# Block sums of the down-projection weights made on the chip by GpSimd instead of in DRAM, in a one-core RetNet/GLA/ConvFFN decoder step

## What is computed

```python
n2 = rmsnorm(h, ln2)
up = n2 @ w_up
u, vv = up[..., :D_FF], up[..., D_FF:]
uc, conv_tail = causal_dwconv(u, conv_prev, conv_w, conv_b)
h = h + (jax.nn.gelu(uc, approximate=False) * vv) @ w_down     # D_FF = 2816, D_MODEL = 1024
```

## Time and profile before

| | us |
|---|---|
| runs of the kernel | 831.44, 833.9, 834.17 (median 833.9) |
| the profiled execution | 830.95 |
| its span | 829.0 |
| PE busy | 816.9 (99%) |
| DVE busy | 590.1 (71%) |
| ACT busy | 375.0 (45%) |
| POOL busy | 219.4 (26%) |
| HBM read, written | 145.31 MB, 58.40 MB |

### The profile page before, as it was taken

How to read it: one execution, slowest core, us unless ns; L and a number is a source line. 1 busy time by engine, 2 the same in 40 slices (tenths; PEclk the granted TensorE clock), 3 DMA queues, 4 the chain that set the end, 5 groups by cost and what they waited for, 6 DMA issues and landing times.

```text
span 829.0 us, 15746 instructions
## 1 busy us (share of the span) xinstructions
PE 816.9 (99%) x6544; PEld 806.2 (97%) x6544; DVE 590.1 (71%) x765; ACT 375.0 (45%) x524; POOL 219.4 (26%) x258
## 2 busy tenths in 40 slices
PE   8999999999999999999999999999999999999996
PEld 8999999999999999999999999999999999999996
DVE  5464678477898886766558877777777756878973
ACT  5553234232354554534343544444434424544574
POOL 4017236444325500000430433333233322000020
PEclk9999999999999999999999999999999999999998
DMA  9769968983325974528899598589699873555522
GB/s 271 215 204 176 277 200 174 189 238 124 110 96 105 202 256 140 173 96 265 149 250 273 91 259 217 155 194 192 247 205 210 223 173 120 181 175 175 175 64 108
DMA packets 167889, 152.27 MB, mean 184 GB/s; under 512 B 6677, under 2 KB 155881, under 8 KB 167804
## 3 DMA queue, kind: packets, MB, share of 16 engines
q1 hardware_dynamic: 121612, 109.73, 42.4%
q0 software_dynamic: 46048, 41.04, 28.9%
q10 hardware_dynamic: 160, 0.53, 0.2%
HBM read 145.31 MB, written 58.40 MB: 246 GB/s over the span
## 4 chain that ended last, share of the span: by engine, by line
PE 93%; DVE 4%; issue 1%; DMA 1%; ACT 0%; SPq 0%; DVEq 0%; ACTq 0%
PE mm L2024 51%; PE ax L2317 14%; PE mm L2431 8%; PE ax L2431 6%; PE ax L2043 6%; PE mm L2317 4%; PE ax L2048 2%; PE mm L2104 1%; DVE grs L1443 1%; DMA x_nat<-in_x_prompt 1%; DVE wlo L1433 1%; PE mm L2036 0%; DVE s0g L1613 0%; DVE ylo L1691 0%; DVE wlo L1703 0%
## 5 line engine op out<-in xcount | busy, mean ns | idle before, releaser
L2024 PE MATMUL mm<-nhi,whi 128*128 128x272 f32 x928 | 196.4, 293 | 0.6 <-ACT gqk L1009 0.6
L2024 PE MATMUL mm<-nhi,wlo 128*128 128x272 f32 x928 | 192.5, 289 | 0.0
L2024 PE MATMUL mm<-nlo,whi 128*128 128x272 f32 x928 | 192.1, 288 | 0.0
L1009 ACT ACTIVATE whi<-raw 128x1024 fp32r<-128x1024 f32 (+3 forms) x112 | 128.5, 1182 | 70.1 <-PE mm L2024 38.5
L2024 PEld LDWEIGHTS mm<-nhi,whi 128*128 128x128 f32 x928 | 146.9, 189 | 2.8 <-issue 1.2
L2024 PEld LDWEIGHTS mm<-nlo,whi 128*128 128x128 f32 x928 | 146.5, 189 | 0.0
L2024 PEld LDWEIGHTS mm<-nhi,wlo 128*128 128x128 f32 x928 | 145.6, 190 | 0.0
L1703 DVE TENSOR_TENSOR wlo<-raw,whi 128x1024 fp32r<-128x1024 f32 (+1 forms) x78 | 84.4, 1123 | 5.9 <-ACT whi L1009 3.4
L1433 DVE TENSOR_TENSOR wlo<-raw,whi 128x2048 fp32r<-128x2048 f32 x27 | 64.7, 2398 | 16.1 <-ACT whi L1009 16.1
L940 POOL DMA_DIRECT2D v_sums<-in_w_up x24 | 30.8, 4229 | 117.4 <-DVE mlo L1774 116.9
L1009 ACT ACTIVATE whi<-ring 128x1408 fp32r<-128x1408 f32 x25 | 34.6, 1382 | 44.1 <-PE ax L2431 24.0
(11 more groups left out here) (390 smaller groups left out, 1989.3 us busy)
## 6 DMA issues: line engine op xcount, KB each, us to landing
raw<-in_w_in SPq DMA_DIRECT2D x36, 512.0 KB, 4.9
raw<-in_w_up SPq DMA_DIRECT2D x36, 512.0 KB, 7.9
ring<-w_sums SPq DMA_DIRECT2D x16, 704.0 KB, 4.2
w_sums<-in_w_down SPq DMA_DIRECT2D x12, 704.0 KB, 10.9
w_sums<-in_w_down POOLq DMA_DIRECT2D x12, 704.0 KB, 10.8
ring<-in_w_down SPq DMA_DIRECT2D x9, 704.0 KB, 4.5
v_sums<-in_w_up SPq DMA_DIRECT2D x24, 256.0 KB, 7.0
v_sums<-in_w_up POOLq DMA_DIRECT2D x24, 256.0 KB, 14.0
```

The source lines that it names most:

```text
L1009: return act.activation(out, in_, func, **kw).then_inc(done, 1)
L2024: ins = pe.matmul(mm[:, 2 * j + a, 0:HALF], w, x[:, kx, HALF * a:HALF * (a + 1)], start=first and n == 0 and m == 0, stop=last and n == le ...
```

## The change

S_1 alone is still built in DRAM (four copies by SP at the first two up-projection units, four accumulating DMAs by POOL). The other three sums are made in SBUF. The blocks (0,0) stay where product 0 read them (`kept[0..3]`: the two `raw` slots and two slots of the region of the ring), and POOL adds a streamed block to each with one `tensor_tensor` of 128x1408: first (0,1), which makes S_3 (product 2), then (1,1), which makes S_2 (product 3), then (1,0), which makes S_4 (product 5). Each add waits until the previous content of `kept[m]` has been split (`lo_ready`) and until the streamed block has landed. The blocks come through a ring of four slots (`ring`, the fourth in the region of the convolution's tiles), in the order of `STREAM`; products 1, 4 and 6 are split straight from that ring, and (1,1) is loaded twice. `kept[3]` takes the last block of product 6. The other edits of the same diff move `osq[0]` and make ACT's first two `fin` rows wait for the last sum, because of the fourth ring slot.

```diff
-RING = 5
+RING = 4
-    ring = [at(f"ring{i}", [P, KH, P], a0 + i * AB) for i in range(RING)]
+    ring = [at(f"ring{i}", [P, KH, P], a0 + i * AB) for i in range(RING - 1)]
+    kept = first[:] + [at(f"kept{i}", [P, KH, P], a0 + (RING - 3 + i) * AB) for i in (2, 3)]
...
-    w_sums = nc.dram_tensor("w_sums", [4, P, MD, KH, P], F32).ap()
+    w_sums = nc.dram_tensor("w_sums", [P, MD, KH, P], F32).ap()
...
+    ring.append(at("ring3", [P, KH, P], f + T))
...
+    STREAM = [("s1", 0), ("s1", 1), ("01", 0), ("s1", 2), ("01", 1), ("s1", 3), ("01", 2), ("01", 3)]
+    STREAM += [(b, m) for b in ("11", "10", "11 last") for m in range(MD)]
...
     def source(u):
-        if u < 3:
-            return first[u], (first2_in, 16)
-        i = (u - 3) % RING
-        return ring[i], (ring_in[i], 16 * ((u - 3) // RING + 1))
+        p, m = divmod(u, MD)
+        if p == 0:
+            return (first[2], (first2_in, 16)) if m == 2 else (kept[3], (kept_in[3], 16))
+        if p in (1, 4, 6):
+            return streamed({1: "s1", 4: "10", 6: "11 last"}[p], m)
+        return kept[m], (sum_made, {2: 0, 3: MD, 5: 2 * MD}[p] + m + 1)
...
+        def stream_load(n):
+            name, m = STREAM[n]
+            if RING <= n < 8 or n == 9:
+                old = STREAM[n - RING]
+                if old[0] == "s1":
+                    sp.wait_ge(lo_ready, U_DOWN + MD + old[1] + 1)
+                else:
+                    sp.wait_ge(sum_made, old[1] + 1)
+            elif n in (8, 10, 11):
+                sp.wait_ge(sum_made, STREAM[n - RING][1] + 1)
+            elif 12 <= n < 16:
+                sp.wait_ge(sum_made, MD + m + 1)
+            elif 16 <= n < 19:
+                sp.wait_ge(lo_ready, U_DOWN + 4 * MD + m + 1)
+                sp.wait_ge(sum_made, 2 * MD + m + 1)
+            elif n == 19:
+                sp.wait_ge(lo_ready, U_DOWN + 5 * MD + m + 1)
...
+        sp.dma_start(kept[3][:, :, :], w_block(0, 0, 3)).then_inc(kept_in[3], 16)
+        for n in range(3):
+            stream_load(n)
+        for j in range(2):
+            sp.wait_ge(drained[j], FD[j])
+        sp.wait_ge(ext_saved, KF)
+        stream_load(3)
+        sp.dma_start(kept[2][:, :, :], w_block(0, 0, 2)).then_inc(kept_in[2], 16)
...
+        for n in range(4, len(STREAM)):
+            stream_load(n)
...
         for i in range(KF // 2):
             up_pair(i)
-            if i < 3:
-                weight_sum(S_3, ((0, 1), (2,), (3,))[i], (0, 1))
...
+            if i == 3:
+                pool.wait_ge(sum_begun, 16 * MD)
+            if i in (3, 4):
+                for m in (2 * (i - 3), 2 * (i - 3) + 1):
+                    pool.dma_start(w_sums[:, m], w_block(1, 1, m), accum_op=ALU.add).then_inc(sum_done, 16)
+
+        def sum_block(m, split_before, block):
+            b, (arrived, count) = streamed(block, m)
+            pool.wait_ge(lo_ready, U_DOWN + split_before + m + 1)
+            pool.wait_ge(arrived, count)
+            pool.tensor_tensor(kept[m][:, :, :], kept[m][:, :, :], b[:, :, :], ALU.add).then_inc(sum_made, 1)
+
+        for m in range(MD):
+            if m == 2:
+                pool.wait_ge(kept_in[2], 16)
+            sum_block(m, 0, "01")
+        for m in range(MD):
+            sum_block(m, 2 * MD, "11")
+        for m in range(MD):
+            sum_block(m, 3 * MD, "10")
...
                 if f >= 2:
                     aux_wait_filled(act, ("y", f - 2))
+                else:
+                    act.wait_ge(sum_made, 3 * MD)
```

More of the change, by code:

```diff
@@ L371, in build @@
     facc = at("facc", [P, NT], f)
-    osq = [at("osq0", [P, NT], f + 3 * T), at("osq1", [P, NT], a0 + 5 * AB + D_MODEL * 4)]
+    ring.append(at("ring3", [P, KH, P], f + T))
+    assert T + AB <= 4544 + 2 * T
+    osq = [at("osq0", [P, NT], 3 * UB + AB), at("osq1", [P, NT], a0 + 5 * AB + D_MODEL * 4)]
+    assert AB + T <= UB
     fin = [at(f"fin{i}", [P, NT], f + (1 + i) * T) for i in range(2)]
@@ L417, in build @@
     part_done, part_added = sem("part_done"), sem("part_added")
-    sum_begun = [sem(f"sum_begun{i}") for i in range(4)]
-    sum_done = [sem(f"sum_done{i}") for i in range(4)]
+    sum_begun, sum_done = sem("sum_begun"), sem("sum_done")
     ring_in = [sem(f"ring_in{i}") for i in range(RING)]
+    kept_in = [None, None, sem("kept_in2"), sem("kept_in3")]
+    sum_made = sem("sum_made")
     first2_in = sem("first2_in")
@@ L490, in piece_at @@
         return (n // MD + 1, n % MD)
-    S_1, S_3, S_2, S_4 = range(4)
-    A_OF = ((0, 0), S_1, S_3, S_2, (1, 0), S_4, (1, 1))
     W_DOWN = A["w_down"][0].rearrange("(k p) n -> p k n", p=P)
@@ L498, in w_block, with streamed @@
         return W_DOWN[:, KH * kh:KH * (kh + 1), P * (MD * mh + m):P * (MD * mh + m + 1)]
-    def source(u):
-        if u < 3:
-            return first[u], (first2_in, 16)
-        i = (u - 3) % RING
-        return ring[i], (ring_in[i], 16 * ((u - 3) // RING + 1))
+    STREAM = [("s1", 0), ("s1", 1), ("01", 0), ("s1", 2), ("01", 1), ("s1", 3), ("01", 2), ("01", 3)]
+    STREAM += [(b, m) for b in ("11", "10", "11 last") for m in range(MD)]
+    def streamed(name, m):
+        n = STREAM.index((name, m))
+        if (name, m) == ("11 last", MD - 1):
+            return kept[3], (kept_in[3], 32)
+        return ring[n % RING], (ring_in[n % RING], 16 * (n // RING + 1))
+    def source(u):
+        p, m = divmod(u, MD)
[4 more added lines that the diff above has]
+        return kept[m], (sum_made, {2: 0, 3: MD, 5: 2 * MD}[p] + m + 1)
     def added(f, h):
@@ L677, in cols @@
             return w[:, 0:4, bass.ds(c, UC)], w[:, 4:8, bass.ds(c, UC)]
-        begun = [(i, m) for i in (S_3, S_1, S_4) for m in range(MD)]
         def begin_sums(n):
-            for i, m in begun[2 * n:2 * n + 2]:
-                sp.dma_start(w_sums[i, :, m], w_block(*{S_1: (0, 1), S_3: (0, 0), S_4: (1, 0)}[i], m)).then_inc(sum_begun[i], 16)
+            for m in (2 * n, 2 * n + 1):
+                sp.dma_start(w_sums[:, m], w_block(0, 1, m)).then_inc(sum_begun, 16)
         gs_copies = [(G_3, (0, 0)), (G_1, (0, 1)), (G_4, (1, 0))]
@@ L732, in _ @@
             load((U_WO + n) % 2, U_WO + n - 1, *cols(w_o, UC * n))
-            if n % 2 == 1:
-                begin_sums(n // 2)
         for n, (kind, i) in enumerate(UPS):
@@ L743, in _ @@
                 block_load(u, kind, w_up, D_FF + UC * i, v_sums[:, i - 1])
-            if kind == "u" and i < 4:
-                begin_sums(2 + i)
+            if kind == "u" and i < 2:
+                begin_sums(i)
         for m in range(2):
@@ L751, in _ @@
         sp.dma_start(first[2][:, :, :], w_block(0, 0, 2)).then_inc(first2_in, 16)
[L753 to L761, removed]
-            else:
-                w = w_block(*A_OF[p], m)
-            sp.dma_start(ring[i][:, :, :], w).then_inc(ring_in[i], 16)
+        def stream_load(n):
[15 more added lines that the diff above has]
+                sp.wait_ge(lo_ready, U_DOWN + 5 * MD + m + 1)
+            if name == "s1":
+                if m == 0:
+                    sp.wait_ge(sum_done, 16 * MD)
+                w = w_sums[:, m]
+            else:
+                w = w_block(int(name[0]), int(name[1]), m)
+            to, (arrived, _) = streamed(name, m)
+            sp.dma_start(to[:, :, :], w).then_inc(arrived, 16)
         for j in range(2):
             sp.wait_ge(filled[j], FD[j])
-        for u in range(3, 3 + RING):
-            ring_load(u)
+        sp.dma_start(kept[3][:, :, :], w_block(0, 0, 3)).then_inc(kept_in[3], 16)
[6 more added lines that the diff above has]
+        sp.dma_start(kept[2][:, :, :], w_block(0, 0, 2)).then_inc(kept_in[2], 16)
         for i in range(3):
@@ L775, in _ @@
             sp.dma_start(O[7][0].rearrange("b r d -> (b r) d")[:, c], tail_nat[r + 2:r + 18, 0:n]).then_inc(conv_out, 16)
-        for u in range(3 + RING, PARTS):
-            ring_load(u)
+        for n in range(4, len(STREAM)):
+            stream_load(n)
         yp = O[0][0].rearrange("(j p) d -> p j d", p=P)
@@ L951, in _ @@
         v_weight_sum(G_4, all_sums, lambda i: v_sum(G_2, i))
[L953 to L958, removed]
         def up_pair(i):
```

## The result

The changed kernel takes 852.7 us (median; 851.6 to 853.1) against 833.9 of the kernel before: a ratio of 1.0234, 95% interval 1.0218 to 1.0250, slower. 851.0 was forecast, with 836 to 861 as the range. The profiled execution took 853.1 us, its span is 850.6 us against 829.0. A fourth run of the kernel before, at 1337.7 us, is left out of its median.

The account below looks back on a forecast made before the run. TensorE alone was taken to bound the kernel from 383 us. 830.95+9.7+8.8 gave 849.5 us on the profiled execution, 852.4 on the median of the runs; the forecast was put between, at 851.0, range 836 to 861.

Parts of the forecast that it names:

- step 1: Up projection: removing 8 of SP's copies and 16 of POOL's DMAs gains 0 us, since TensorE doesn't wait there.
- step 5: Down projection, other edits: loads, the S_1 block and the `fin` rows stay hidden, 0 us; slowest landing would cost 3.2 us.
- What the engines do to each other: DVE's and POOL's two-input SBUF instructions wait for each other wholly, longer waiter first; DVE with a PSUM input doesn't wait.
- step 2: Twelve POOL adds of 1408 elements: 3.15 us each, holding the port 3.0 us; other estimates 2.61 and 3.49 us.
- step 3: Sums 5 to 12, down projection: port holds make cycles of 4.54 to 5.74 us against 4.13, together +9.7 us.
- step 4: Sums 1 to 4, waiting for blocks: +1.1 at part 4, then +2.5, then +5.2 us, together +8.8 us.
- its own sign: Down projection: the prediction would be wrong if PEclk, TensorE's granted clock, left 1.00 there.
- rival 5: Down projection: POOL's add takes 4.5 us or more, or waits lower TensorE's clock; 858 to 866 us, chance 0.08.
- the likeliest case: Down projection: port waits between POOL's adds and DVE as worked out, 841 to 857 us, chance 0.75.
- POOL alone waiting: Down projection: POOL gets the port only in DVE's gaps, nothing is late; 831 to 834 us, chance 0.07.
- a late block: Down projection: port waits mostly fall into idle time, a late block costs 3.2 us; 834 to 837 us, chance 0.05.
- A gain from less DRAM traffic: From 450 us on, 17 MB less copied and added speeds the matmuls; 828 us or less, chance 0.05.

Follow-up runs that it names:

- the first experiment: The changed kernel with each of POOL's twelve adds cut to the first of its 11 tiles: 833.6 us, ratio 1.0012 to the kernel before.

## Why the prediction was right

**What bounds the kernel; the up projection.** Right. The chain before is TensorE alone, and the kernel with hardly any adds shows 0 for everything else, as step 1 and step 5 had it.

**What the engines do to each other.** Right, and shown: exclusion in both directions (POOL 4.22, DVE 4.02 us in the same round), turns by who waits longer (POOL ahead of the combination issued at 723.61, DVE in between POOL's half adds), the adds with an operand in PSUM untouched at 0.71 us, and no exclusion by writes alone.

**The add itself, step 2.** 3.15 us expected, 3.23 at the least measured: the estimate by the two nearest rows held. The bound of 2.61 us was far off for these operands; a time near it (2.54) came with another instruction, a subtraction with one range as both operands.

**The rounds, step 3.** With a full piece 5.74 us expected, 5.78 measured (753.14 to 758.92). The sum over sums 5 to 12 was 9.7 us; from part 8 to part 16 the trace has 787.18-742.87 = 44.3 us, where before it was 33.4 (from 715.85 and half of the 33.34 us of parts 4 to 11, 732.52, to 765.93), so 10.9. Of these, 3.6 us are the two slow parts, so the waits proper are 7.3: the waits given to parts 9, 10, 13 and 14 (0.3, 0.4, 0.4 and 1.6) were mostly hidden under the slow parts. Alone the last eight adds cost 9.5 to 9.7 us (10.5 by the trace).

**The first four, step 4.** 8.8 expected, 8.0 by the trace (part 2 to part 8: 32.9 against 25.0 us), 10.3 to 11.6 alone (9.4 by the trace; the slow part 8 adds its 1.7 us there). The places differ a little: the first add came 0.6 us ahead of part 3's low weights and not behind them, so part 3 was late (by 0.9), not part 4; before part 6 it was 2.6 us for 2.5; the 5.2 us put before part 7 came in two, 2.0 and 1.8 us before parts 7 and 8, 3.8 in all.

**The sum.** The sum gave 852.4 on the median of the kernel before; 852.7 was measured. Placing the forecast between the two bases was a needless hedge: the measured difference of medians is 18.8 us against the sum's 18.5. That it is so close is in part luck: the first four adds came out 0.8 us under their term, the last eight 1.2 over. And the sum had no term for the clock. Waits proper add up to 15.3 us (the 18.9 less 3.6), against 18.5 in the walk; the two slow parts make up the rest. These two errors belong together, as the slow parts stand where TensorE would have waited for DVE anyway: with the clock up the down projection is only 0 to 0.4 us shorter.

**The clock.** Here the prediction was wrong by its own sign: PEclk did leave 1.00 in the down projection. The fall was named in rival 5 with 4.1 us for a spell: it happened twice, in the likeliest case itself, at 1.8 us each, for a spell covers less than one part. The walk had waits of 1.6 to 5.2 us before parts 6, 7, 11, 12, 14 and 15, so the likeliest case should have named the fall, with a small net cost. The other sign that was off: parts 12 to 16 start 5.9, 4.4, 5.8 and 5.5 us apart, where 5.7 was given for all.

**Rivals.** POOL alone waiting and a late block are out by the trace and by the first experiment. A gain from less DRAM traffic is out by the same.

## What to carry to other kernels

An idle engine isn't free to use if it shares a port with the engine that is the next bound. Ask of POOL work beside a busy DVE: does it read SBUF, are DVE's instructions two-input ones in SBUF, how long is one POOL instruction, and how large is DVE's margin? Here the margin was 1.0 us; twelve holds of 0.3 us cost nothing, of 1.7 us 3 us, of 3.1 us 19 us, and the same twelve adds made by DVE 2.9 us. If POOL must read, short instructions cost less than long ones (847.0 us in place of 852.4 with each add in two).

## What was not expected of the hardware

TensorE's granted clock fell to its lower level after waits of only 1.8 to 2.6 us in a row of parts, with 4.4 us of matmuls between them. I had thought of one long wait as the place. In the kernel with the first four adds it fell at part 6 already, after the 2.6 us; in the kernel with five filled waits it did not fall after 2.3 us before part 12. A POOL `tensor_tensor` of 1408 elements took 2.54 us as a subtraction with one range as both operands and 3.22 us as an addition with two. About 1.2 us of matmuls of no use in only five of the waits kept the granted clock at 1.00 from 700 to 800 us, past a later wait that was left empty.
